# First adaptive norm of a 512-token network: modulation blocks summed along rows in PSUM, x/rms split off and computed ahead

## The chip, the cores and the metric

One core of one Trainium2 chip. The metric is the device time of one execution in microseconds (us); the kernel before has a median of 2411.16 us over three runs (2410.75 to 2412.59).

## What is computed

Two transformer-like networks one after the other on x (512 tokens, width 1024), four layers in all. The change touches only the beginning, the modulated norm of layer 0 and what the first projections need of it:

```python
def adaln(c, w_mod, b_mod):
    mod = jax.nn.silu(c) @ w_mod + b_mod
    return jnp.split(mod, 6, axis=-1)
...
def modulate(x, g, shift, scale):
    return rmsnorm(x, g) * (1.0 + scale[:, None, :]) + shift[:, None, :]
...
    sh_m, sc_m, g_m, sh_f, sc_f, g_f = adaln(c, mod_w, mod_b)
    h = modulate(x, norm_mix, sh_m, sc_m)
    (a_gate, a_x, q, kc, vc, ks, vs, kw, vw, gts) = _split(h @ w_in, IN0_SIZES)
```

c is one vector of 1024, so the modulation is a vector times a 1024 x 6144 matrix per layer. The first norm needs shift and scale, 16 blocks of 128 outputs (8 of each).

## The kernel before, in words

Activations lie transposed: partition = feature within a block of 128, eight blocks k, 512 tokens along the row. A product in fp32 quality is made of three products of rounded parts (`three`, L717: high x high, high x low, low x high), so every activation h is kept as h_hi and h_lo, and every weight panel (128 outputs x 1024 inputs) as w_hi and w_lo. SP loads raw panels into a ring of four; ScalarE copies the high part (L1233); GpSimd subtracts the low part (L640); TensorE multiplies (L718 to L720). The program is written out by hand for each of five engines, and semaphores order them.

The beginning: SP's queue issues the column constants, x, batch 0 of the modulation blocks (`first_mods`, 2 MB), raw panels 0 to 2, batches 1 to 3, raw panel 3. A batch n holds four blocks of 128 outputs: shift for k = 2n and 2n + 1, scale for the same two. ScalarE squares x (L1369), GpSimd adds the squares in pairs (L677), TensorE sums them over partitions (L952) and later spreads 1/rms over all partitions into bank 5 (`spread`, L820). ScalarE takes the root (L1374), VectorE its reciprocal (L1654).

In each batch TensorE multiplies block 0 with silu(c) as columns (L728, eight narrow products). VectorE sums blocks 1 to 3 over k in a chain of eight operations in PSUM (L1899, L1906), 384 elements each with a drain between, and TensorE sums the result over partitions (L732). `first_h(n)` (L1977) then adds the bias (L1980), makes the gain (L1984), scales x (tn, L1990), and after ScalarE's rounding (h_hi, L1259) subtracts the low part (L1995), for two k.

The order on VectorE is batch 0, reciprocal, batch 1, `first_h(0)`, `first_h(1)`, batches 2 and 3, `first_h(2)`, `first_h(3)`. On TensorE it is:

```python
            first_batch(0)
            spread(0, bank[5], QB)
            first_batch(1)
            by_k(0, h_hi, h_lo, 0, (0, 1, 2, 3))
            first_batch(2)
            first_batch(3)
            by_k(0, h_hi, h_lo, 0, (4, 5, 6, 7))
```

`by_k` (L735) multiplies panels 0, 1 and 2 side by side, nine products for each k as h_lo comes in. Behind it come panel 3, the products of `hidden(0)` (L978, from VectorE's blocks, L2052, and the weights w1), panel 4, the gates of the recurrence (L969, from VectorE's convolution, L2014 and L2017), and so on. ScalarE issues the loads of crow (a row of c on all partitions, for later blocks), peT, w2, w1, w_small and cmask after its last h_hi.

Of the kernel before, what the change touches and what calls it, by code (L numbers as in the profile page):

```python
# [13 lines left out]
F32 = mybir.dt.float32  # L14
# [105 lines left out]
def build(nc, A):  # L120
    with ExitStack() as ctx:
# [15 lines left out]
        FIRST_BANK = [bank[7], bank[4], bank[3], bank[7]]  # L137
        CHAIN = bank[6]
# [13 lines left out]
        modacc = sb("modacc", [P, 2])  # L152
        cols = sb("cols", [P, N_COLS])
# [34 lines left out]
        def s(name, shape, kib):  # L188
            return sb(name, shape, at=sx + int(kib * 1024))
# [5 lines left out]
        modsum = s("modsum", [P, 4, P], 16)  # L195
# [75 lines left out]
        crow_landed = sem("crow_landed")  # L271
        crow_ready = sem("crow_ready")
        first_landed = [sem(f"first_landed{n}") for n in range(BATCHES)]
        first_added = sem("first_added")
# [361 lines left out]
        def _(pool):  # L636
# [41 lines left out]
            split_from(0, P_OUT0 + 2)  # L678
# [37 lines left out]
        def _(pe):  # L716
# [17 lines left out]

# [212 lines left out]
            pe.wait_ge(csil_ready, 1)  # L947
            pe.wait_ge(filled, 1)
# [273 lines left out]
        def _(act):  # L1222
# [158 lines left out]
            act.wait_ge(mod_used, BATCHES)  # L1381
# [43 lines left out]
            for p in range(P_OUT0):  # L1425
# [188 lines left out]
        def _(dve):  # L1614
# [280 lines left out]
            def weighted(blocks_, n, to, used, between=None):  # L1895

                w = blocks_.rearrange("p n (k m) -> p n k m", m=P)
                part = CHAIN[:, 0:n * P].rearrange("p (n m) -> p n m", m=P)
                dve.tensor_scalar(part, w[:, :, 0, :], csil[:, 0:1], None, MUL)  # L1899
                for k in range(1, KB):  # L1900
                    if k == KB // 2 and between is not None:
                        between()
                    dve.drain()
                    if k == KB - 1 and used is not None:
                        dve.wait_ge(mod_used, used)
                    m = dve.scalar_tensor_tensor(out=part if k < KB - 1 else to, in0=w[:, :, k, :], scalar=csil[:, k:k + 1],  # L1906
                                                 in1=part, op0=MUL, op1=ADD)
                m.then_inc(mod_summed, 1)
                dve.drain()

            def sum_first(n, between=None):
                dve.wait_ge(first_landed[n], 16)
                weighted(first_mods[n][:, 1:4, :], 3, modsum[:, 1:4, :], n if n else None, between)
# [63 lines left out]
            def first_h(n):  # L1977

                dve.wait_ge(mod_used, n + 1)
                dve.tensor_tensor(by_part(modv[:, 0:2 * KB], n), FIRST_BANK[n][:, 0:4].rearrange("p (w k) -> p w k", w=2),  # L1980
                                  by_part(cols[:, COLS["modb"]:COLS["modb"] + 2 * KB], n), ADD).then_inc(first_added, 1)
# [3 lines left out]
                                         in1=cols[:, at:at + 2], op0=ADD, op1=MUL)  # L1985
                if n == 0:
                    dve.wait_ge(rstd_ready, 1)
                dve.drain()
                for k in (2 * n, 2 * n + 1):
                    dve.scalar_tensor_tensor(out=tn[:, k % 2, :], in0=x[:, k, :], scalar=gain(0, k), in1=bank[5][:, :],  # L1990
                                             op0=MUL, op1=MUL).then_inc(t_ready, 1)
                dve.drain()
# [569 lines left out]
```

## Time and profile before

| | us |
|---|---|
| median of three runs | 2411.16 |
| profiled execution | 2408.87 |
| its span | 2407.1 |
| TensorE busy | 2348.3 (98%) |
| VectorE busy | 1348.5 (56%) |
| ScalarE busy | 936.6 (39%) |
| GpSimd busy | 1123.0 (47%) |

The span is what the trace covers; the execution's own time is 1.8 us longer. Busy shares are averages over the whole program and say nothing of a single stage: for that one cuts the span into windows and reads the timelines. PE is TensorE's matmul, PEld its weight load, DVE VectorE, ACT ScalarE, POOL GpSimd, SP the engine that issues the panel loads; "ACTq" is an issue of a DMA by ScalarE's queue. Starts are counted from the start of the span. A row with x8 merges eight like instructions, its second number being the time from the first's start to the last's end, or nearly so.

### The profile page before, as it was taken

The page shows a single profiled execution, that of the slowest core. Times are in us where ns is not written, and L with a number is a line of the kernel's source. Part 1 is how long each engine was busy: PE and PEld are TensorE (multiplying, and loading weights), DVE is VectorE, ACT ScalarE, POOL GpSimd, SP SyncE. Part 2 cuts the span into 40 slices and gives each one's busy share as a digit, 9 for nine tenths or more (in the row PEclk, how much of TensorE's full clock was granted, in tenths as well). Part 3 has the DMA queues.
Part 4 walks back from the last instruction along what each step waited for, and adds up shares of the span by engine and source line. Part 5 has one row for each costly group of instructions (what it writes and reads, how often), then busy time and mean ns, then how long its engine had stood idle before and what let it go on. Part 6 is the DMA issues. An engine that isn't in the chain of part 4 may idle for free.

```text
span 2407.1 us, 33622 instructions
## 1 busy us (share of the span) xinstructions
PE 2348.3 (98%) x11781; PEld 1911.1 (79%) x11781; DVE 1348.5 (56%) x2132; ACT 936.6 (39%) x1495; POOL 1123.0 (47%) x529
## 2 busy tenths in 40 slices
PE   7999999999999999999999999999999999999998
PEld 6777788888776778888888678888888968888886
DVE  6786777772448651111158857263567474736455
ACT  3467332222336733222244544222256383322222
POOL 2346354554536535444446534444454473444443
PEclk9999999999999999999999999999999999999999
DMA  7530446653322023322332132323232202232322
GB/s 292 205 123 2 158 169 213 247 209 114 113 71 71 28 70 105 96 96 96 96 100 94 53 105 90 104 87 104 88 121 92 92 19 79 88 105 88 105 87 79
DMA packets 70095, 262.01 MB, mean 109 GB/s; under 512 B 7904, under 2 KB 8416, under 8 KB 68960
## 3 DMA queue, kind: packets, MB, share of 16 engines
q1 hardware_dynamic: 66816, 251.01, 30.8%
q10 hardware_dynamic: 3168, 9.50, 1.1%
q8 instruction: 72, 1.18, 0.2%
q14 instruction: 39, 0.32, 0.0%
HBM read 258.38 MB, written 2.10 MB: 108 GB/s over the span
## 4 chain that ended last, share of the span: by engine, by line
PE 88%; DVE 5%; issue 2%; POOL 1%; DMA 1%; ACT 1%; POOLq 1%; DVEq 0%; SPq 0%; ACTq 0%
PE bank L718 26%; PE bank L720 26%; PE bank L719 26%; PE bank L890 2%; PE bank L909 2%; PE bank L878 2%; POOL w_lo L640 1%; DMA first_mods<-in_first 1%; DVE acc L1646 1%; POOLq L706 1%; DVE bank L2254 1%; POOL prob L658 1%; PE bank L820 0%; DVE bank L1906 0%; DVE prob L1825 0%
## 5 line engine op out<-in xcount | busy, mean ns | idle before, releaser
L640 POOL TENSOR_TENSOR w_lo<-raw,w_hi 128x1024 fp32r<-128x1024 f32 x378 | 943.9, 2506 | 1178.9 <-ACT w_hi L1233 1176.9
L718 PE MATMUL bank<-h_hi,w_hi 128*128 128x512 f32 x1760 | 695.4, 395 | 12.3 <-DVE h_lo L1693 7.8
L719 PE MATMUL bank<-h_lo,w_hi 128*128 128x512 f32 x1760 | 688.9, 391 | 0.0
L720 PE MATMUL bank<-h_hi,w_lo 128*128 128x512 f32 x1760 | 688.9, 391 | 0.0
L1233 ACT ACTIVATE w_hi<-raw 128x1024 fp32r<-128x1024 f32 x378 | 392.6, 1051 | 426.8 <-PE bank L720 387.3
L718 PE MATMUL bank<-g_hi,w_hi 128*128 128x512 f32 x1072 | 421.1, 393 | 0.0
L720 PE MATMUL bank<-g_hi,w_lo 128*128 128x512 f32 x1072 | 420.9, 393 | 0.0
L719 PE MATMUL bank<-g_lo,w_hi 128*128 128x512 f32 x1072 | 417.3, 389 | 0.0
L718 PEld LDWEIGHTS bank<-h_hi,w_hi 128*128 128x128 f32 x1760 | 333.0, 189 | 93.4 <-DVE h_lo L1693 8.7
L720 PEld LDWEIGHTS bank<-h_hi,w_lo 128*128 128x128 f32 x1760 | 332.7, 189 | 70.4
L719 PEld LDWEIGHTS bank<-h_lo,w_hi 128*128 128x128 f32 x1760 | 333.2, 189 | 69.2 <-issue 0.8
L719 PEld LDWEIGHTS bank<-g_lo,w_hi 128*128 128x128 f32 x1072 | 201.3, 188 | 45.4
L720 PEld LDWEIGHTS bank<-g_hi,w_lo 128*128 128x128 f32 x1072 | 201.3, 188 | 45.2
L718 PEld LDWEIGHTS bank<-g_hi,w_hi 128*128 128x128 f32 x1072 | 201.5, 188 | 41.5 <-issue 0.2
L1785 DVE TENSOR_TENSOR prod<-silu,bank 128x512 f32<-128x512 f32 x44 | 30.2, 687 | 256.3 <-PE bank L720 253.8
L1919 DVE SCALAR_TENSOR_TENSOR modraw<-modraw,crow 128x1024 f32<-128x1024 f32 x80 | 160.4, 2034 | 22.1 <-DMA modraw<-in_blocks 21.3
L1298 ACT ACTIVATE g_hi<-prod 128x512 f32 x66 | 41.7, 632 | 303.9 <-DVE prod L1785 200.1
L658 POOL TENSOR_TENSOR prob<-prob,stat 128x256 f32<-128x256 f32 (+3 forms) x96 | 118.6, 1253 | 61.7 <-DVE stat L1834 42.7
L1709 DVE SCALAR_TENSOR_TENSOR x<-bank,plain,x 128x512 f32<-128x512 f32 x64 | 47.6, 749 | 155.7 <-PE bank L720 155.6
L1318 ACT ACTIVATE prob<-prob,stat 128x384 f32<-128x384 f32 (+2 forms) x192 | 105.9, 557 | 18.1 <-DVE stat L1825 17.5
L1709 DVE SCALAR_TENSOR_TENSOR x<-bank,modv,x 128x512 f32<-128x512 f32 x64 | 47.7, 749 | 112.9 <-PE bank L720 111.7
L1825 DVE CUSTOM_DVE_ANT_0 prob<-bank,mask 128x384 f32<-128x384 f32 (+2 forms) x192 | 86.0, 486 | 29.7 <-PE bank L878 28.5
(295 smaller groups left out, 2461.0 us busy)
## 6 DMA issues: line engine op xcount, KB each, us to landing
raw<-in_panels SPq DMA_DIRECT2D x378, 512.0 KB, 3.5
modraw<-in_blocks SPq DMA_DIRECT2D x80, 512.0 KB, 3.7
first_mods<-in_first SPq DMA_DIRECT2D x4, 2048.0 KB, 21.9
x<-in_x SPq DMA_DIRECT2D x1, 2048.0 KB, 8.3
w<-in_w ACTq DMA_DIRECT2D x1, 2048.0 KB, 8.7
out<-yout ACTq DMA_DIRECT2D x8, 256.0 KB, 2.2
mask<-in_causal ACTq DMA_DIRECT2D x1, 1024.0 KB, 5.0
mask<-in_dilated ACTq DMA_DIRECT2D x1, 1024.0 KB, 7.5
```

What stands on the lines that cost most here:

```text
L640: pool.tensor_tensor(w_lo[:, slot, :], raw[:, slot, :], w_hi[:, slot, :].bitcast(F32), ALU.subtract)\
L658: m = pool.tensor_tensor(both, both, stat[:, 2, u:u + 2].rearrange("p (b o) -> p b o", o=1) .broadcast_to((P, 2, w)), ALU.mult)
L718: pe.matmul(out, w_h, m_h, start=start, stop=False)
L719: pe.matmul(out, w_h, m_l, start=False, stop=False)
L720: return pe.matmul(out, w_l, m_h, start=False, stop=stop)
L878: m = pe.matmul(score_bank(run, n, b)[:, off:off + P * (i + 1)], q_of(run, i, c, b), k_of(run, i, c, br, b), start=True, stop=True)
L890: m = pe.transpose(bank[2 + b][:, P * j:P * j + P], prob[:, PROB_SLOT[n % PROB_STEPS], b, P * j:P * j + P], ident[:, :])
L1233: act.activation(w_hi[:, slot, :], raw[:, slot, :], ACT.Copy).then_inc(hi_ready, 1)
L1318: act.activation(row, row, ACT.Exp, bias=stat[:, 0, u:u + 1], scale=-1.0, accum_out=stat[:, 1, u:u + 1]).then_inc(exp_ready, 1)
L1709: dve.scalar_tensor_tensor(out=x[:, n, :], in0=bank[p % RING][:, :], scalar=scale_by, in1=x[:, n, :], op0=MUL, op1=ADD).then_inc(bank_free, 1)
L1825: dve.tensor_tensor_reduce(row_of(n, b, off, w), score_bank(run, n, b)[:, off:off + w], mask[:, i, 0:w], -SCALE, HIGHEST, ADD, ALU.min, st ...
L1919: dve.scalar_tensor_tensor(out=modraw[:, w, :], in0=modraw[:, w, :], scalar=1.0, in1=crow[:, :], op0=MUL, op1=MUL, accum_out=modacc[:, w:w ...
```

## The change

silu(c) is spread once over all partitions as a row in banks 6 and 7 (`spread_crow`, eight products with the identity). The modulation blocks are stored transposed (an output per partition), so VectorE gets a whole output with one multiplication along the row and an accumulator, in two halves of 512 since a bank holds 512 (`sum_rows`); of batches 1 to 3 block 0 stays with TensorE (`first_block`), of batch 0 all four are VectorE's. The sums over partitions (L732) are gone. x/rms is made once without the gain: k = 0, 1 by VectorE, k = 2 to 7 by GpSimd from a copy of 1/rms in SBUF. ScalarE applies gain and shift twice, to h_hi (rounded) and to the exact value in bank 3 or 5, and VectorE subtracts the two (`first_low`). ScalarE's table of roots is loaded ahead by a root of one. Its DMA issues come after the last exact value, lruw's among them, and crow is copied out of PSUM instead of loaded.

```diff
-        FIRST_BANK = [bank[7], bank[4], bank[3], bank[7]]
-        CHAIN = bank[6]
+        FIRST_COLUMN, FIRST_H = bank[4], (bank[3], bank[5])
+        CROW = (bank[6], bank[7])
...
-            split_from(0, P_OUT0 + 2)
+            split_from(0, 3)
+            pool.wait_ge(rb0_ready, 1)
+            for k in range(2, KB):
+                pool.tensor_tensor(sq0[:, k, :], x[:, k, :], rb0[:, :], ALU.mult).then_inc(xr_pool_ready, 1)
+            split_from(3, P_OUT0 - 1)
...
-            def first_batch(n):
+            def first_block(n):
 
                 pe.wait_ge(first_landed[n], 16)
-                if n == 3:
-                    pe.wait_ge(first_added, 1)
+                if n > 1:
+                    pe.wait_ge(mods_ready, n)
                 for k in range(KB):
-                    pe.matmul(FIRST_BANK[n][:, 0:1], first_mods[n][:, 0, P * k:P * k + P], csil[:, k:k + 1],
-                              start=(k == 0), stop=(k == KB - 1))
-                pe.wait_ge(mod_summed, n + 1)
-                for w in range(1, 4):
-                    m = pe.matmul(FIRST_BANK[n][:, w:w + 1], modsum[:, w, :], ones[:, 0:1], start=True, stop=True)
+                    m = pe.matmul(FIRST_COLUMN[:, n:n + 1], first_mods[n][:, 0, P * k:P * k + P], csil[:, k:k + 1],
+                                  start=(k == 0), stop=(k == KB - 1))
                 m.then_inc(mod_used, 1)
+
+            def spread_crow():
+
+                for k in range(KB):
+                    m = pe.matmul(CROW[k // 4][:, P * (k % 4):P * (k % 4) + P], csil[:, k:k + 1].broadcast_to((P, P)),
+                                  ident[:, :], start=True, stop=True)
+                m.then_inc(crow_spread, 1)
...
             pe.wait_ge(csil_ready, 1)
+            spread_crow()
...
-            first_batch(0)
             spread(0, bank[5], QB)
-            first_batch(1)
-            by_k(0, h_hi, h_lo, 0, (0, 1, 2, 3))
-            first_batch(2)
-            first_batch(3)
+            first_block(1)
+            by_k(0, h_hi, h_lo, 0, (0, 1))
+            first_block(2)
+            by_k(0, h_hi, h_lo, 0, (2, 3))
+            first_block(3)
             by_k(0, h_hi, h_lo, 0, (4, 5, 6, 7))
...
+            def first_high():
+
+                for k in range(KB):
+                    if k == 4:
+                        split_hi(3)
+                    act.wait_ge(mods_ready, k // 2 + 1)
+                    if k < 2:
+                        act.wait_ge(xr_ready, k + 1)
+                    else:
+                        act.wait_ge(xr_pool_ready, k - 1)
+                    act.activation(h_hi[:, k, :], sq0[:, k, :], ACT.Identity, bias=shift(0, k), scale=gain(0, k))\
+                        .then_inc(h_hi_ready, 1)
+                    if k == 1:
+                        act.wait_ge(rb0_ready, 1)
+                    elif k >= 2:
+                        act.wait_ge(h_lo_ready, k - 1)
+                    act.activation(FIRST_H[k % 2][:, :], sq0[:, k, :], ACT.Identity, bias=shift(0, k), scale=gain(0, k))\
+                        .then_inc(h32_ready, 1)
...
+            act.activation(root[:, 6 * QB - 1:6 * QB], one, ACT.Sqrt)
...
+            first_high()
+            act.wait_ge(h32_ready, KB)
             act.dma_start(lruw[:, :, :, :], A["lruw"]).then_inc(lru_landed, 16)
-            h_high(0)
-            act.dma_start(crow[:, :], A["crow"]).then_inc(crow_landed, 16)
...
-                    act.wait_ge(crow_landed, 16)
-                    act.activation(crow[:, :], crow[:, :], ACT.Silu).then_inc(crow_ready, 1)
+                    for half in range(2):
+                        m = act.activation(crow[:, T * half:T * half + T], CROW[half][:, :], ACT.Copy)
+                    m.then_inc(crow_ready, 1)
...
+            def sum_rows(n, ws):
+
                 dve.wait_ge(first_landed[n], 16)
-                weighted(first_mods[n][:, 1:4, :], 3, modsum[:, 1:4, :], n if n else None, between)
+                for w in ws:
+                    for half in range(2):
+                        row = first_mods[n][:, w, T * half:T * half + T]
+                        m = dve.scalar_tensor_tensor(out=row, in0=row, scalar=1.0, in1=CROW[half][:, :],
+                                                     op0=MUL, op1=MUL, accum_out=modhalf[:, half, w:w + 1])
+                if ws[-1] == 3:
+                    m.then_inc(mod_summed, 1)
...
+            def first_mod(n):
+
+                dve.drain()
+                if n:
+                    dve.wait_ge(mod_used, n)
+                    dve.tensor_copy(modhalf[:, 0, 0:1], FIRST_COLUMN[:, n:n + 1])
+                    dve.drain()
+                dve.tensor_tensor(modhalf[:, 0, :], modhalf[:, 0, :], modhalf[:, 1, :], ADD)
+                dve.drain()
...
+            def first_low(k):
+
+                dve.wait_ge(h_hi_ready, k + 1)
+                dve.wait_ge(h32_ready, k + 1)
+                dve.tensor_tensor(h_lo[:, k, :], FIRST_H[k % 2][:, :], h_hi[:, k, :].bitcast(F32), SUB).then_inc(h_lo_ready, 1)
+
+            dve.wait_ge(crow_spread, 1)
+            sum_rows(0, (0, 1, 2, 3))
             invert_root(0)
-            sum_first(1)
-            first_h(0)
-            first_h(1)
-            sum_first(2)
-            sum_first(3)
-            first_h(2)
-            first_h(3)
+            first_mod(0)
+            dve.wait_ge(rstd_ready, 1)
+            for k in range(2):
+                dve.tensor_tensor(sq0[:, k, :], x[:, k, :], bank[5][:, :], MUL).then_inc(xr_ready, 1)
+            dve.tensor_copy(rb0[:, :], bank[5][:, :]).then_inc(rb0_ready, 1)
+            for n in range(1, BATCHES):
+                ahead = (1,) if n == 1 else (1, 2)
+                sum_rows(n, ahead)
+                first_low(2 * n - 2)
+                first_low(2 * n - 1)
+                sum_rows(n, tuple(w for w in (1, 2, 3) if w not in ahead))
+                first_mod(n)
+            first_low(KB - 2)
+            first_low(KB - 1)
```

On VectorE, from the landing of batch 1 to the low parts of k = 0 and 1, before (modsum is the chain's result, tn the scaled x, bank7 batch 0's sums):

```order
L1899 TENSOR_SCALAR bank6<-first_mods1_80,csil_64 128x384 [waits first_landed1]
L1906 SCALAR_TENSOR_TENSOR bank6<-first_mods1_80,csil_64,bank6 128x384 x6
L1906 SCALAR_TENSOR_TENSOR modsum_84<-first_mods1_80,csil_64,bank6 128x384 [waits mod_used]
L1980 TENSOR_TENSOR modv_61<-bank7,cols_58 128x2x2 [waits mod_used]
L1984 SCALAR_TENSOR_TENSOR gains_62<-modv_61,cols_58 128x2
L1990 SCALAR_TENSOR_TENSOR tn_89<-x_49,gains_62,bank5 128x512 [waits rstd_ready]
L1990 SCALAR_TENSOR_TENSOR tn_89<-x_49,gains_62,bank5 128x512
L1995 SCALAR_TENSOR_TENSOR h_lo_51<-tn_89,modv_61,h_hi_50 128x512 [waits h_hi_ready] x2
```

and with the change (modhalf holds the half sums, sq0 x/rms, rb0 the copy of 1/rms, banks 3 and 5 the exact values):

```order
L2030 TENSOR_TENSOR sq0_84<-x_49,bank5 128x512 [waits rstd_ready]
L2030 TENSOR_TENSOR sq0_84<-x_49,bank5 128x512
L2031 COPY rb0_85<-bank5 128x512
L1933 SCALAR_TENSOR_TENSOR first_mods1_81,modhalf_58<-first_mods1_81,bank6 128x512 [waits first_landed1]
L1933 SCALAR_TENSOR_TENSOR first_mods1_81,modhalf_58<-first_mods1_81,bank7 128x512
L2022 TENSOR_TENSOR h_lo_51<-bank3,h_hi_50 128x512 [waits h32_ready,h_hi_ready]
L2022 TENSOR_TENSOR h_lo_51<-bank5,h_hi_50 128x512 [waits h32_ready,h_hi_ready]
L1933 SCALAR_TENSOR_TENSOR first_mods1_81,modhalf_58<-first_mods1_81,bank6 128x512 [waits first_landed1]
```

The low parts of k = 0 and 1 now stand behind two half rows of batch 1 instead of behind its whole chain, and the rest of batch 1 comes after them.

On ScalarE, between the squares and the first high part, before:

```order
L1233 ACTIVATE w_hi_53<-raw_52 128x1024 [waits raw_landed0]
L1233 ACTIVATE w_hi_53<-raw_52 128x1024 [waits raw_landed1]
L1233 ACTIVATE w_hi_53<-raw_52 128x1024 [waits raw_landed2]
L1374 ACT_TABLE_LOAD
L1374 ACTIVATE root_65<-bank0 128x1 [waits sums_ready]
```

and with the change:

```order
L1401 ACT_TABLE_LOAD
L1401 ACTIVATE root_66<-plain_64 128x1
L1247 ACTIVATE w_hi_53<-raw_52 128x1024 [waits raw_landed0]
L1247 ACTIVATE w_hi_53<-raw_52 128x1024 [waits raw_landed1]
L1247 ACTIVATE w_hi_53<-raw_52 128x1024 [waits raw_landed2]
L1406 ACTIVATE root_66<-bank0 128x1 [waits sums_ready]
```

The table load has moved from behind the three splits to ahead of them.

## Rows read from the trace of the kernel before

**Rows 1.** Windows: us, busy of each engine (instructions), granted clock, DMA.

```profile
0.00:70.00 70.00, 53.84 (x260) 48.27 (x261) 46.76 (x96) 26.70 (x38) 23.72 (x16) 0.95 0.74 290
...
1000.00:2407.00 1407.00, 1387.98 (x6751) 1140.03 (x6749) 732.01 (x1043) 523.25 (x762) 651.74 (x296) 0.99 0.27 90
```

**Rows 2.** Timeline of TensorE, first 75 us: start, us, line, operation.

```profile
12.20 6.96 PE L952 MATMUL bank<-ones,sq 128*128 128x1 f32 x32 [12.20 <-POOL sq L677]
...
23.71 2.05 PE L820 MATMUL bank<-ident,root 128*128 128x128 f32 x8
25.55 3.41 PE L728 MATMUL bank<-csil,first_mods 128*128 128x1 f32 x16
...
32.05 0.79 PE L718 MATMUL bank<-h_hi,w_hi 128*128 128x512 f32 x1 [1.45 <-DVE h_lo L1995]
...
36.06 0.42 PE L718 MATMUL bank<-h_hi,w_hi 128*128 128x512 f32 x1
...
42.23 1.84 PE L728 MATMUL bank<-csil,first_mods 128*128 128x1 f32 x16
...
50.33 0.79 PE L718 MATMUL bank<-h_hi,w_hi 128*128 128x512 f32 x1 [1.46 <-DVE h_lo L1995]
...
59.95 0.39 PE L718 MATMUL bank<-h_hi,w_hi 128*128 128x512 f32 x1
...
65.49 3.71 PE L978 MATMUL bank<-w,blocks 128*64 128x128 f32 x32
```

**Rows 3.** Timeline of VectorE, first 75 us.

```profile
14.55 0.62 DVE L1899 TENSOR_SCALAR bank<-first_mods,csil 128x384 f32<-128x384 f32 x1 [4.23 <-DMA first_mods<-in_first]
...
23.20 0.62 DVE L1899 TENSOR_SCALAR bank<-first_mods,csil 128x384 f32<-128x384 f32 x1 [1.95 <-DMA first_mods<-in_first]
...
29.46 0.16 DVE L1984 SCALAR_TENSOR_TENSOR gains<-modv,cols 128x2 f32<-128x2 f32 x1
29.71 1.41 DVE L1990 SCALAR_TENSOR_TENSOR tn<-x,gains,bank 128x512 f32<-128x512 f32 x2
...
58.87 5.60 DVE L2052 TENSOR_TENSOR blocks<-bank,peT 64x496 f32<-64x496 f32 x8 [4.04 <-PE bank L720]
...
71.83 0.68 DVE L1622 COPY axp<-bank 128x512 f32<-128x512 f32 x1
```

**Rows 4.** Timeline of ScalarE, first 75 us.

```profile
19.38 1.28 ACT L1374 ACT_TABLE_LOAD   x1
20.67 0.17 ACT L1374 ACTIVATE root<-bank 128x1 f32<-128x1 f32 x1
...
30.49 1.38 ACT L1259 ACTIVATE h_hi<-tn,modv 128x512 fp32r<-128x512 f32 x2 [9.46 <-DVE tn L1990]
...
52.99 0.33 ACTq L1378 DMA_DIRECT2D crow<-in_crow  x1
...
54.33 0.44 ACTq L1382 DMA_DIRECT2D w<-in_w  x1
```

**Rows 5.** Timeline of GpSimd, first 90 us.

```profile
10.78 4.94 POOL L677 TENSOR_TENSOR sq<-sq 128x512 f32<-128x512 f32 x4 [10.26 <-ACT sq L1369]
16.88 6.98 POOL L640 TENSOR_TENSOR w_lo<-raw,w_hi 128x1024 fp32r<-128x1024 f32 x3 [1.16 <-ACT w_hi L1233]
```

**Rows 6.** VectorE's groups, shapes apart (busy, mean ns); last row min/median/max ns.

```profile
L1919 DVE SCALAR_TENSOR_TENSOR modraw<-modraw,crow 128x1024 f32<-128x1024 f32 x80 | 160.4, 2034 | 22.1 <-DMA modraw<-in_blocks 21.3 <-issue 0.3
...
L1825 DVE CUSTOM_DVE_ANT_0 prob<-bank,mask 128x512 f32<-128x512 f32 x48 | 32.1, 686 | 10.9 <-PE bank L878 10.2 <-issue 0.4
...
L1785 DVE TENSOR_TENSOR prod<-silu,bank 128x512 f32<-128x512 f32 x44 | 30.2, 687 | 256.3 <-PE bank L720 253.8 <-issue 2.5
...
L1906 DVE SCALAR_TENSOR_TENSOR bank<-first_mods,csil,bank x24: 621/622/625, 15.3 to 46.1; 128x384 f32<-128x384 f32 x24
```

**Rows 7.** DMA issues, first 100 us: KB, us to landing.

```profile
w<-in_w ACTq DMA_DIRECT2D x1, 2048.0 KB, 8.7
```

**Rows 8.** Windows, as in the first group.

```profile
48.00:50.00 2.00, 0.88 (x5) 0.79 (x4) 1.87 (x3) 1.23 (x2) 0.00 (x0) 0.50 0.00 0
```

More of the change, by code:

```diff
@@ L152, in build @@
         modacc = sb("modacc", [P, 2])
+        modhalf = sb("modhalf", [P, 2, 4])
         cols = sb("cols", [P, N_COLS])
@@ L194, in build @@
         sq0 = s("sq0", [P, KB, T], 0)
-        modsum = s("modsum", [P, 4, P], 16)
+        rb0 = s("rb0", [P, T], 16)
         sq = s("sq", [P, 2, T], 0)
@@ L270, in build @@
         mod_landed = [sem(f"mod_landed{n}") for n in range(2)]
-        crow_landed = sem("crow_landed")
+        crow_spread = sem("crow_spread")
         crow_ready = sem("crow_ready")
         first_landed = [sem(f"first_landed{n}") for n in range(BATCHES)]
-        first_added = sem("first_added")
+        mods_ready = sem("mods_ready")
+        xr_ready = sem("xr_ready")
+        xr_pool_ready = sem("xr_pool_ready")
+        rb0_ready = sem("rb0_ready")
+        h32_ready = sem("h32_ready")
         consts_landed = sem("consts_landed")
@@ L1255, in h_high @@
                 for k in range(KB):
-                    if r == 0 and k == 4:
-                        split_hi(3)
-                    act.wait_ge(t_ready, KB * H_OF[r] + k + 1)
-                    act.activation(h_hi[:, k, :], tn[:, k % 2, :], ACT.Identity, bias=shift(r, k)).then_inc(h_hi_ready, 1)
+                    act.wait_ge(t_ready, KB * (H_OF[r] - 1) + k + 1)
+                    act.activation(h_hi[:, k, :], tn[:, k % 2, :], ACT.Identity, bias=shift(r, k)).then_inc(h_hi_ready, 1)
+            def first_high():
+                for k in range(KB):
+                    if k == 4:
+                        split_hi(3)
+                    act.wait_ge(mods_ready, k // 2 + 1)
[11 more added lines that the diff above has]
+                        .then_inc(h32_ready, 1)
             def project(p0, r):
@@ L1893, in set_gains @@
                 dve.drain()
[L1895 to L1911, printed above, removed]
-                dve.wait_ge(first_landed[n], 16)
-                weighted(first_mods[n][:, 1:4, :], 3, modsum[:, 1:4, :], n if n else None, between)
+            def sum_rows(n, ws):
+                dve.wait_ge(first_landed[n], 16)
+                for w in ws:
[5 more added lines that the diff above has]
+                    m.then_inc(mod_summed, 1)
             def sum_pair(m, landed):
@@ L1975, in by_part @@
                 return v_.rearrange("p (w k) -> p w k", w=2)[:, :, 2 * n:2 * n + 2]
[L1977 to L1981, printed above, removed]
+            def first_mod(n):
[6 more added lines that the diff above has]
+                dve.drain()
+                dve.tensor_tensor(by_part(modv[:, 0:2 * KB], n), modhalf[:, 0, :].rearrange("p (w k) -> p w k", w=2),
+                                  by_part(cols[:, COLS["modb"]:COLS["modb"] + 2 * KB], n), ADD)
+                if n == 0:
+                    dve.memset(modhalf[:, 1, 0:1], 0.0)
                 dve.drain()
@@ L1984, in first_h @@
                 dve.scalar_tensor_tensor(out=gains[:, 2 * n:2 * n + 2], in0=modv[:, KB + 2 * n:KB + 2 * n + 2], scalar=1.0,
[L1985 to L1991, printed above, removed]
@@ L1992, in first_h @@
-                dve.drain()
-                for k in (2 * n, 2 * n + 1):
-                    dve.wait_ge(h_hi_ready, k + 1)
-                    dve.scalar_tensor_tensor(out=h_lo[:, k, :], in0=tn[:, k % 2, :], scalar=shift(0, k),
-                                             in1=h_hi[:, k, :].bitcast(F32), op0=ADD, op1=SUB).then_inc(h_lo_ready, 1)
-                dve.drain()
-            dve.wait_ge(csil_ready, 1)
-            sum_first(0)
-            invert_root(0)
-            sum_first(1)
@@ L2003, in _ @@
[L2003 to L2008 removed]
+                                         in1=cols[:, at:at + 2], op0=ADD, op1=MUL).then_inc(mods_ready, 1)
+            def first_low(k):
+                dve.wait_ge(h_hi_ready, k + 1)
+                dve.wait_ge(h32_ready, k + 1)
+                dve.tensor_tensor(h_lo[:, k, :], FIRST_H[k % 2][:, :], h_hi[:, k, :].bitcast(F32), SUB).then_inc(h_lo_ready, 1)
@@ L2009, in _ @@
+            first_low(KB - 2)
+            first_low(KB - 1)
+            dve.drain()
             dve.memset(axp[:, :, 0:TAPS_LRU - 1], 0.0)
@@ L2479, in laid_out @@
     mods = np.concatenate([panel_arrays(f["l0_mod_w"]), panel_arrays(f["l1_mod_w"])])
-    out["first"] = np.stack([mods[[2 * n, 2 * n + 1, KB + 2 * n, KB + 2 * n + 1]] for n in range(BATCHES)]).transpose(0, 2, 1, 3)
     by_row = np.concatenate([f["l0_mod_w"].T, f["l1_mod_w"].T]).reshape(2 * MOD, P, D)
+    first_of = [[2 * n, 2 * n + 1, KB + 2 * n, KB + 2 * n + 1] for n in range(BATCHES)]
+    batches = [np.stack([by_row[b] if n == 0 or w else mods[b] for w, b in enumerate(of)]) for n, of in enumerate(first_of)]
+    out["first"] = np.stack(batches).transpose(0, 2, 1, 3)
     out["blocks"] = by_row[MOD_FIRST:]
-    out["crow"] = np.broadcast_to(f["c"], (P, D))
     def c(v_):
```

1 line of the change is left out of this document (removed).

## The prediction

> **What bounds the kernel now.** I read the windows first. After the first stage TensorE is the bound: from 1000 us on it is busy 1387.98 of 1407 us, but in the first 70 us only 53.84 [rows 1]. All that the change touches lies in those 70 us, and everything behind them hangs on TensorE's progress, so a microsecond by which the first real panel work ends earlier comes off the end.
>
> TensorE's timeline [rows 2] shows what it does there: column sums, narrow products of the modulation blocks, the spread of 1/rms, then panels 0 to 2 block by block in k. The first of these products starts at 32.05, a second pause lies between 42.23 and 50.33, and panel 3 starts at 59.95. That last moment is my mark. VectorE's timeline [rows 3] says who holds it up. Batch 0 begins when it lands (14.55), batch 1 when it lands (23.20), and only after all of batch 1 does it scale x (29.71), although the gains of k = 0, 1 hang on batch 0 alone. Later it sums batches 2 and 3 in one go before k = 4 is begun. The first stage is a chain of VectorE work with TensorE waiting.
>
> **The change, step by step.** The price of a half-row sum (128x512, one input in SBUF, one in PSUM, with an accumulator) is not in the trace. The nearest row is L1825, a custom operation with the same operands and an accumulator, 686 ns [rows 6]. The multiply that feeds prod from SBUF and PSUM takes 687 ns beside GpSimd's splits. Two operations one behind the other are some 0.05 to 0.09 us closer than their durations say (L1990: 1.41 us for two of 745 ns, [rows 3]). I take 0.66 us per half row. Upper bound: L1919, the same instruction over 1024 elements with both inputs in SBUF, means 2034 ns [rows 6], so 1.02 us per half; lower bound 0.61.
>
> Start of the norm. VectorE: 14.55 + 8 x 0.66 = 19.85. ScalarE's table load (1.28 us at 19.38, [rows 4]) goes ahead of the splits, into its wait for raw panel 0, so the roots start at 19.4, after the column sums (12.20 + 6.96 = 19.16, [rows 2]), and end at 19.75 instead of 21.03. Reciprocal by 20.1. The narrow products of batch 0 no longer stand ahead of the spread, so it runs from 20.15 and takes 2.05 [rows 2]: 22.2, against 25.76. The eight products of silu(c)'s row would cost about 4.1 (twice a spread), but stand where TensorE has nothing else to do until 12.20: nothing. The three small operations of batch 0's gains cost 0.26 each [rows 3], done before 22.2.
>
> k = 0. Multiply by 1/rms 22.3 to 23.0. ScalarE then writes high part and exact value: 0.73 + 0.65 (1.38 for two, [rows 4]) = 24.45. Writing to PSUM has no row; ScalarE's nearest are these. The Trainium skill (ScalarE: Activation LUTs, "Step-by-step: what each stage is for") calls PSUM the faster destination; by that the exact value would come a little sooner, no run here shows it. VectorE meanwhile: second product, copy of 1/rms (24.3), one row of batch 1 (25.6), low part 0.7: 26.3. TensorE has block 1's column in front: from 23.20 (landing) 3.5 us at the slow pace [rows 2], 26.7. So the products start at **26.8**, 5.25 earlier, bound by TensorE itself.
>
> The pace. In the trace the first nine products take 4.0 us (32.05 to 36.06), the rest 0.228 each [rows 2]. So k = 0, 1 (18 products) take 6.05: 32.85. Block 2's column at the fast pace 1.84: 34.7. VectorE: low(1) 26.95, four half rows 29.6, four small operations and a drain 1.15: 30.75; four half rows of batch 2 33.4; low(2) 34.1, ready before 34.7 (ScalarE's 1.4 us lie under the half rows). k = 2, 3: 18 x 0.228 = 4.1, 38.8. VectorE: low(3) 34.75, two half rows 36.1, small ones 37.2, so block 3's column runs 38.8 to 40.65. Four half rows 39.85, low(4) 40.5: k = 4, 5 from 40.65 to 44.75. VectorE: low(5) 41.2, two half rows 42.5, small ones 43.65; ScalarE two writes 45.05; low(6) 45.75. Here VectorE is late by 1.0. k = 6, 7: 45.8 + 4.1 = **49.9**. Mark: 59.95 - 49.9 = **10.05 us earlier**.
>
> GpSimd's six multiplies cost 1.24 each (4.94 for four additions, [rows 5]): from 24.3, k = 2 at 25.6, needed at 30.8; the last at 31.7. Behind them waits the split of panel 3 (2.3 us, a third of 6.98), whose low part is needed only at 49.9: hidden, with over 10 us to spare. The split's raw load and the later loads in SP's queue wait for the same low parts as before, at about the same time.
>
> What is late next. ScalarE's DMA issues follow its last write: 46.4 instead of 52.99 [rows 4], and lruw now goes ahead of the others instead of crow. w1 (2 MB) was issued at 54.33 and took 8.7 [rows 7], landing at 63.0, 10.0 after the first issue. Its first reader starts at 65.49, with 2.5 us to spare. That slack shrinks: the mark moves by 10.05, the issues by 6.6. The reader could start at 49.9 + 5.5 = 55.45; w1 lands at 46.4 + 10.0 = 56.4, or 55.7 with the 0.25 MB less ahead of it. A new wait of 0.25 to 0.95, I take **0.6**. The next one: VectorE's blocks take 5.6 [rows 3] and start at 49.7 when peT lands, the small weights come at about 56.3, the convolution ends near 64 against panel 4's end at 65.1, where before it had 3 us (71.83, [rows 3]). No wait, but thin.
>
> Sum: -10.05 + 0.6 = **-9.4 us**. Profiled execution 2408.87 to 2399.5; the median of the three runs stands 2.3 above it, so 2411.16 - 9.4 = **2401.8**.
>
> **Rivals.**
> (a) The clock drops in the gaps. Between 48 and 50 us the granted clock is 0.50, the lower of the two levels, after some 4.5 us of nothing but narrow products [rows 8], and 50.33 starts slowly. The gaps now are 1.85, 1.85 and 1.0 us, all shorter. If the clock fell nevertheless at both columns, k = 2, 3 would end at 40.65, the slow column takes it to 42.5 or 44.2, and 36 products with a slow start need 10.0: mark at 52.5 to 54.2, gain 5.7 to 7.4, time near 2404.5. The Trainium skill (TensorE: Matmul & The Clock Gate, "What's actually happening") lets the clock fall after an idle window that runs freely; the trace agrees that a long narrow stretch does it. By it a gap this short should be safe, unless narrow products and pauses together count as idle.
> (b) VectorE is the bound throughout, since half rows cost more. Adding up its chain gives the mark as 32.8 + 26 p (26 half rows of p us; 49.95 at 0.66). At p = 0.85 the gain is 5.05 less the 0.6: within the 0.2% (4.8 us), which is what a measurement of this kernel can tell from no change. At the upper bound 1.02 the mark is 59.3, nothing gained: 2411. Against: every operation with a PSUM input in rows 6 is near 0.69.
> (c) Slower. GpSimd holds VectorE up at the SBUF port, PSUM input or not. L1919's mean of 2034 shows such holds where both inputs are in SBUF. GpSimd works from 16.88 to 23.86 (6.98, [rows 5]) and then its 7.4 us of multiplies, which stand beside half rows now and beside nothing before. If every operation of VectorE waited for one of GpSimd, it would lose up to 7.0 + 7.4 = 14.4: mark at 64.3, and the end at 2415 to 2416. It decides from 10 us of loss on. Against it: L1906 reads SBUF and PSUM and is 621 to 625 ns over all 24, those beside the splits of 16.88 among them [rows 6]. The Trainium skill (SBUF — State Buffer, "Who interferes with whom") says a VectorE instruction with at most one SBUF input doesn't contend; the trace agrees, with these 621 to 625 ns. By it this rival would be out.
> (d) The gain is given back behind the mark: w1, w_small or the convolution 3 to 5 us late, or VectorE and GpSimd falling into worse step in the attention. Then 2405 to 2407. For it: three slacks shrink at once.
>
> **Chances.** Forecast 0.70, (a) 0.14, (b) 0.06 with half of it inside 0.2%, (c) 0.03, (d) 0.07 with half inside. Faster by over 0.2%: 0.90; within: 0.07; slower: 0.03. Range: below, no VectorE delay at k = 6 and no wait for w1 give a mark of 48.9, -11.05 us, 2400.1, and 1 us for the spread of the runs: 2399.0. Above, (a) and half of (d): 2406.4.
>
> **What would show it.** The first h_hi,w_hi product at 26.8; L1933 near 0.69 us; pauses of TensorE before k = 2 and 4 under 0.3 us and before k = 6 about 1; panel 3 at 49.9; hidden(0) waiting for w1 by 0.6; the granted clock at 1.00 from 31 us on. Half rows of over 0.8 us would mean (b) or (c), products of 0.43 us after 34 us (a), an unchanged distance from mark to end is what I count on, and any growth of it over 1.5 us is (d).

## The result: 10.5 us slower, though the first stage ends 6.9 us earlier

| | before | after |
|---|---|---|
| median of five runs, us | 2411.62 | 2422.10 |
| lowest to highest | 2410.75 to 2413.54 | 2420.76 to 2427.55 |
| span of the profiled execution | 2407.1 | 2419.0 |

The ratio is 1.0042 (95% interval 1.0031 to 1.0054). The forecast was 2401.8.

The windows of the changed kernel's trace answer to [rows 1]; two stretches are added, in which TensorE has nothing but products of g_hi and g_lo (columns: from and to, length, busy us and instructions of PE, PEld, DVE, ACT, POOL, granted clock, DMA share, GB/s).

```profile
0.00:70.00 70.00, 55.61 (x264) 47.25 (x264) 50.42 (x123) 32.71 (x49) 31.76 (x23) 0.85 0.75 292
400.00:420.00 20.00, 20.00 (x87) 16.09 (x86) 15.33 (x19) 3.19 (x3) 9.06 (x4) 1.00 0.78 270
1890.00:1900.00 10.00, 10.00 (x85) 10.00 (x85) 5.02 (x5) 2.00 (x2) 3.46 (x2) 1.00 0.18 55
1000.00:2407.00 1407.00, 1394.06 (x6733) 1137.91 (x6731) 723.65 (x1032) 521.56 (x759) 652.13 (x296) 1.00 0.27 89
```

The same two stretches of the kernel before:

```profile
400.00:420.00 20.00, 20.00 (x89) 16.43 (x88) 15.03 (x20) 3.18 (x3) 8.10 (x4) 1.00 0.76 259
1890.00:1900.00 10.00, 10.00 (x91) 10.00 (x90) 6.76 (x4) 2.01 (x2) 5.20 (x2) 1.00 0.34 107
```

TensorE is busy without a gap and its clock is granted in full in both, yet 87 of its instructions fall into 20 us where 89 did, and 85 into 10 us where 91 did. Over the last 1407 us it is busy 6.08 us more for 18 instructions fewer. So the loss is not waiting: the products themselves follow each other more slowly. The durations of single products don't show it well (0.39 to 0.40 us each, since they overlap); the distance from start to start does. Rows of TensorE's timeline, first of the kernel before, then of the changed one:

```profile
399.91 0.39 PE L718 MATMUL bank<-g_hi,w_hi 128*128 128x512 f32 x1
...
419.82 0.39 PE L718 MATMUL bank<-g_hi,w_hi 128*128 128x512 f32 x1
```

```profile
399.95 0.39 PE L727 MATMUL bank<-g_hi,w_hi 128*128 128x512 f32 x1
...
420.25 0.40 PE L727 MATMUL bank<-g_hi,w_hi 128*128 128x512 f32 x1
```

Between the two rows lie 87 products each time: 19.91 / 87 = 228.9 ns before, 20.30 / 87 = 233.3 ns after. I call this distance the pace. Taken so over the whole trace (9264 products of panels), the pace is 226.7 ns in both kernels where h_hi and h_lo are the moving operand and nothing interrupts. Where g_hi and g_lo move it is 228.9 and 233.3. And where g_hi is held still and 256 columns of w_hi move (near 1900 us) it is 113.3 and 120.0. Added up from 300 us on, the slower pace is 15.4 us (over the whole trace the mean with g_hi and g_lo moving is a little lower than in these rows, 229.0 and 233.0).

**The first stage** did about what was forecast. TensorE's timeline after, answering to [rows 2]:

```profile
4.56 3.78 PE L744 MATMUL bank<-ident,csil 128*128 128x128 f32 x16 [4.56 <-ACT csil L1395]
12.16 6.96 PE L966 MATMUL bank<-ones,sq 128*128 128x1 f32 x32 [3.82 <-POOL sq L682]
...
27.73 0.80 PE L727 MATMUL bank<-h_hi,w_hi 128*128 128x512 f32 x1 [1.05 <-DVE h_lo L2022]
...
36.77 0.50 PE L727 MATMUL bank<-h_hi,w_hi 128*128 128x512 f32 x1 [0.77 <-DVE h_lo L2022]
...
43.66 0.50 PE L727 MATMUL bank<-h_hi,w_hi 128*128 128x512 f32 x1 [0.83 <-DVE h_lo L2022]
...
48.84 0.50 PE L727 MATMUL bank<-h_hi,w_hi 128*128 128x512 f32 x1 [0.82 <-DVE h_lo L2022]
...
53.07 0.39 PE L727 MATMUL bank<-h_hi,w_hi 128*128 128x512 f32 x1
...
59.30 3.71 PE L992 MATMUL bank<-w,blocks 128*64 128x128 f32 x32 [0.64 <-DMA w<-in_w]
```

The granted clock's mean is 0.85 over these 70 us, and 0.95 in [rows 1]. A window of the kernel before, then of the changed one:

```profile
20.00:28.00 8.00, 8.00 (x40) 8.00 (x39) 4.18 (x9) 1.02 (x5) 3.86 (x2) 1.00 1.01 423
```

```profile
20.00:28.00 8.00, 5.74 (x25) 5.36 (x26) 7.77 (x13) 2.90 (x4) 5.87 (x4) 0.50 1.00 427
```

The record stays at 0.50 until 32 us and is 1.00 from 34 us on, where I forecast 1.00 from 31. Yet the column sums take 6.96 us in both kernels, and the first products begin 0.43 us apart in both (27.73 to 32.16 here, 32.05 to 36.06 before), nearly twice the later 0.23. So the two records differ where the work does not, and no time of this stage hangs on that. The mark (panel 3) is at 53.07 instead of 59.95: 6.9 us earlier, where 10.05 were forecast. hidden(0) starts at 59.30 instead of 65.49 and waits 0.64 us for w1, as forecast (0.6). TensorE pauses before each of the four groups of k, and the row says for whom: VectorE. Only the last of these pauses, before k = 6, was forecast, at about 1. Its timeline after, without the half rows (L1933), answers to [rows 3]; GpSimd's, beneath it, to [rows 5]:

```profile
19.85 1.67 DVE L2007 TENSOR_TENSOR modhalf<-modhalf 128x4 f32<-128x4 f32 x1
21.60 2.22 DVE L2009 TENSOR_TENSOR modv<-modhalf,cols 128x4 f32<-128x4 f32 x1
...
31.20 1.00 DVE L2007 TENSOR_TENSOR modhalf<-modhalf 128x4 f32<-128x4 f32 x1
32.27 1.17 DVE L2009 TENSOR_TENSOR modv<-modhalf,cols 128x4 f32<-128x4 f32 x1
...
38.94 1.15 DVE L2007 TENSOR_TENSOR modhalf<-modhalf 128x4 f32<-128x4 f32 x1
40.17 0.17 DVE L2009 TENSOR_TENSOR modv<-modhalf,cols 128x4 f32<-128x4 f32 x1
...
45.83 0.16 DVE L2007 TENSOR_TENSOR modhalf<-modhalf 128x4 f32<-128x4 f32 x1
```

```profile
16.83 6.97 POOL L645 TENSOR_TENSOR w_lo<-raw,w_hi 128x1024 fp32r<-128x1024 f32 x3 [1.12 <-ACT w_hi L1247]
25.94 7.49 POOL L686 TENSOR_TENSOR sq<-x,rb 128x512 f32<-128x512 f32 x6 [2.13 <-DVE rb L2031]
37.67 2.40 POOL L645 TENSOR_TENSOR w_lo<-raw,w_hi 128x1024 fp32r<-128x1024 f32 x1 [4.25 <-ACT w_hi L1247]
```

Additions of four numbers per partition take 1.0 to 2.2 us while GpSimd works, and each of the five ends where an operation of GpSimd ends: 23.82 beside 23.80, 33.44 beside 33.43, 40.09 beside 40.07, and the other two, taken apart from the merged rows, 21.52 beside 21.50 and 32.20 beside 32.18. At 40.17 and 45.83 GpSimd is idle, and such an addition takes 0.16 to 0.17. They read two tensors in SBUF. The half rows, with one input in SBUF and one in PSUM, are not touched:

```profile
L1933 DVE SCALAR_TENSOR_TENSOR first_mods<-first_mods,bank 128x512 f32<-128x512 f32 x26 | 16.3, 682 | 4.3 <-DMA first_mods<-in_first 4.3
```

So there are two things to settle: why products that the change doesn't touch go slower, and whether the small additions are what the first stage lacks.

### The profile page after: what moved, and what is told of

Its sections match the earlier page's. It is cut to its first block, busy times and chain, and to the rows that moved or that the text cites. A ratio compares the mean times of both kernels' runs of the same rounds, so it can differ in the third digit from the quotient of the medians.

```text
span 2419.0 us, 33590 instructions
## 1 busy us (share of the span) xinstructions
PE 2358.0 (97%) x11757; PEld 1906.9 (79%) x11757; DVE 1340.6 (55%) x2155; ACT 942.2 (39%) x1504; POOL 1130.2 (47%) x535
## 4 chain that ended last, share of the span: by engine, by line
PE 85%; DVE 6%; issue 3%; DMA 2%; POOL 1%; ACT 1%; POOLq 1%; DVEq 1%; SPq 0%; ACTq 0%
PE bank L727 26%; PE bank L728 26%; PE bank L729 26%; PE bank L903 2%; PE bank L922 2%; PE bank L891 2%; DMA modraw<-in_blocks 1%; POOL w_lo L645 1%; DVE acc L1678 1%; POOLq L715 1%; DVE bank L2287 1%; DMA raw<-in_panels 1%; DVE modraw L1942 1%; POOL prob L663 1%; DVE xc L2050 1%
## 5 line engine op out<-in xcount | busy, mean ns | idle before, releaser
L728 PE MATMUL bank<-g_lo,w_hi 128*128 128x512 f32 x1072 | 423.2, 395 | 0.0
```

Of the source, the lines that this page charges most:

```text
L728: pe.matmul(out, w_h, m_l, start=False, stop=False)
```

## The experiments

**First four: is it the place in TensorE's instruction stream?** My first theory for the pace. The changed kernel issues fewer instructions on TensorE, so all code behind stands elsewhere in the stream, and the pace differed in stretches that are not loops. Each kernel gets extra narrow products where TensorE is idle, 12 of them making up for the difference:

```diff
+            pe.wait_ge(filled, 1)
+            for _ in range(12):          # or 1, or 4
+                pe.matmul(bank[4][:, 8:9], ones[:, :], ones[:, 0:1], start=True, stop=True)
             pe.wait_ge(csil_ready, 1)
```

> Twelve narrow products more on TensorE in the changed kernel, before csil is ready, where TensorE has nothing to do; their results are read by nobody. They bring the number of TensorE's instructions ahead of everything behind the first stage back to about that of the kernel before. Theory L (the place of the straight-line code in TensorE's instruction stream sets its pace): first stage as in the changed kernel, panel 3 at 53.1 +- 0.3 us; the 192 products from about 377 us on go at 228.9 ns each, no longer 233.2, the narrower ones of attention(2) at 113.3 instead of 120.0; time 2404 to 2409. Rival W (the changed work itself, or where tiles and loads now stand in time, slows the later products): pace stays 233.2 and 120.0, time 2420 to 2424.

> The same with one narrow product more instead of twelve. Theory L: the first stage is unchanged, and the pace of the straight-line stretches may differ from 233.2 ns in some or all of them; time anywhere from 2404 to 2424, by how many of them change. Rival W: 2420 to 2424 and 233.2 ns.

> Four narrow products more in the kernel before, in the same idle time of TensorE. Theory L: panel 3 at 59.95 as before, the pace of the straight-line stretches may leave 228.9 ns; time 2408 to 2426. Rival W: 228.9 ns, 2410.7 to 2413.5 as before.

> Twelve narrow products more in the kernel before. Theory L: panel 3 at 59.95, the pace of the straight-line stretches may leave 228.9 ns; time 2408 to 2426. Rival W: 228.9 ns, 2410.7 to 2413.5.

| kernel | median, us | ratio to before (95%) | pace with g_hi moving / held |
|---|---|---|---|
| after, 12 more | 2423.78 | 1.0047 (1.0030 to 1.0064) | 233.3 / 120.0 |
| after, 1 more | 2423.18 | 1.0040 (1.0026 to 1.0054) | 233.3 / 120.0 |
| before, 4 more | 2413.47 | 1.0002 (0.9993 to 1.0012) | 228.9 / 113.3 |
| before, 12 more | 2414.59 | 1.0004 (0.9994 to 1.0014) | 228.9 / 113.3 |

Theory L falls: no padding moves the pace in any of these stretches. The rival W, that the changed work or its moment slows the products, is not yet shown either.

**Second four: the SBUF address.** What the slow stretches have in common is the tile: they read g_hi and g_lo. These are allocated behind modacc, and the change puts a new tile, modhalf, between. It is 32 bytes per partition, rounded up to 64, so that g_hi and all behind it stand 64 B higher, while h_hi and the weights' ring stand as before. This one line of the diff moved the tiles, and the prediction never looked at it. Four kernels move g_hi in steps of 64 B, in either version, and with it all tiles allocated behind the moved one; no instruction differs otherwise:

```diff
-        modhalf = sb("modhalf", [P, 2, 4])        # e2_after_same_place
 ...
         sp = sb("sp", [P, 6, LC])
+        modhalf = sb("modhalf", [P, 2, 4])        # and modacc too: e2_after_m64
```
```diff
         modacc = sb("modacc", [P, 2])
+        hole = sb("hole", [P, 16])                # e2_before_p64; behind modhalf: e2_after_p64
```

> The new small tile modhalf (64 B per partition) stands behind all others instead of ahead of cols, so that every tile behind it, g_hi and g_lo (the moving operands of the down and out panels) and attention's tiles among them, has the SBUF address that it has in the kernel before; nothing else differs from the changed kernel. Theory A (the SBUF address of the moving tiles sets the pace): the 192 products from about 377 us on at 228.9 ns, no longer 233.2; attention(2)'s at 113.3 instead of 120.0; panel 3 at 53.1; time 2405 to 2410, below the kernel before. Rival W (the changed work itself slows the later products): 233.2 and 120.0, 2420 to 2424.

> The kernel before with 64 B per partition left empty behind modacc, so that the tiles behind it have the addresses of the changed kernel; no instruction differs otherwise. Theory A: 233.2 ns and 120.0 from 380 us on, panel 3 at 59.95, time 2424 to 2429 (15 us of pace more). Rival W: 228.9 and 113.3, 2410.7 to 2413.5.

> As e2_after_same_place, and modacc (64 B) behind all others too: the tiles behind stand 64 B lower than in the kernel before. Theory A says that the pace depends on the address, not by how much: between 226.7 ns (that of the products whose moving tile is h_hi, 128 B past a multiple of 16 KB, as g_hi now is past a multiple of 1 KB) and 233.2; if 226.7, the time is 2398 to 2405. Rival W: 233.2, 2420 to 2424.

> The changed kernel with a further 64 B left empty behind modhalf: g_hi 64 B higher than there. Theory A: the pace is another than 233.2 ns or the same, by the period in the address; if it only matters whether the address is a multiple of 128 B (as in the changed kernel) or not (as before), 228.9 and 2405 to 2410. Rival W: 233.2, 2420 to 2424.

| kernel | g_hi against before | median, us | ratio to before (95%) | pace moving / held |
|---|---|---|---|---|
| after, same place | 0 | 2408.84 | 0.9982 (0.9972 to 0.9992) | 228.9 / 113.3 |
| before, +64 B | +64 | 2427.16 | 1.0051 (1.0034 to 1.0068) | 233.3 / 120.0 |
| after, -64 B | -64 | 2404.40 | 0.9957 (0.9941 to 0.9974) | 226.7 / 120.0 |
| after, +64 B | +128 | 2422.43 | 1.0033 (1.0020 to 1.0046) | 233.3 / 117.8 |

W, which forecast unchanged paces in all four, falls by the first three. Theory A holds in the first two, whose paces and times it named. For the last two it left the pace open: 226.7 was its lower bound for the third, and the guess that all depends on whether g_hi stands at a multiple of 128 B (228.9 for the fourth) missed. A hole of 64 B in the kernel before, without an instruction changed, costs 13.9 us (2427.16 against 2413.25) and brings the changed kernel's paces. With its tiles back in place the changed kernel is faster than before. The window of 400 to 420 us, of the kernel before with its hole, then of the changed one with g_hi 64 B lower:

```profile
400.00:420.00 20.00, 20.00 (x87) 16.12 (x86) 15.00 (x19) 3.18 (x3) 8.22 (x4) 1.00 0.71 236
```

```profile
400.00:420.00 20.00, 20.00 (x90) 16.57 (x89) 14.63 (x19) 3.19 (x3) 8.17 (x4) 1.00 0.78 265
```

87 instructions in the first, as in the changed kernel; 90 in the second. Such a count is coarse, since products overlap and those cut by an edge are counted too. By the starts the second kernel has 226.7 ns here, the pace that its h_hi panels have.

**Last four: one address or a distance, and the small additions.** Two are the kernel before, one with modacc behind all other tiles, so that g_hi stands 64 B lower, one with all tiles 64 B higher; the third rewrites the small additions in the changed kernel with g_hi 64 B lower; the fourth is its base.

```diff
-        base = (nc.sbuf_base + 63) // 64 * 64
+        base = (nc.sbuf_base + 63) // 64 * 64 + 64        # e3_before_all64
```
```diff
-                dve.tensor_tensor(modhalf[:, 0, :], modhalf[:, 0, :], modhalf[:, 1, :], ADD)        # e3_m64_cols
-                dve.drain()
-                dve.tensor_tensor(by_part(modv[:, 0:2 * KB], n), ..., by_part(cols[...], n), ADD)
+                for w in range(4):
+                    dve.tensor_scalar(to, modhalf[:, 0, w:w + 1], modhalf[:, 1, w:w + 1], cols[:, own:own + 1], ADD, ADD)
                 dve.drain()
-                dve.scalar_tensor_tensor(out=gains[:, 2 * n:2 * n + 2], ...)
+                for k in (2 * n, 2 * n + 1):
+                    dve.tensor_scalar(gains[:, k:k + 1], modv[:, KB + k:KB + k + 1], 1.0, cols[:, at:at + 1], ADD, MUL)
```

> The kernel before with modacc behind all other tiles, so that g_hi and all tiles behind it stand 64 B lower, as in e2_after_m64; nothing of the change. Theory A (address of the tiles that TensorE reads sets its pace): down panels at 226.7 ns for 228.9, the 384 narrower products of the last stretch at 120.0 for 113.3; 2880 products or so gain 2.2 ns (6.3 us), 384 lose 6.7 (2.6 us): 2407 to 2410 where the kernel before gives 2411 to 2413. Rival (address and change act only together): as the kernel before.

> The kernel before with every tile 64 B higher, x, h_hi and the weights' ring too: distances between tiles as before, every address another. Theory A1 (what counts is how the moving and the stationary tile stand to each other): 226.7 ns where h_hi is read, 228.9 for g_hi, 113.3 at 1900 us, and the time of before, 2410 to 2415. Theory A2 (what counts is each tile's own address): paces of 228.9 to 233 where h_hi is read, too, over some 5000 products: 2420 to 2450.

> e2_after_m64 with the small operations of the gains written without a second tensor in SBUF: each column is one tensor_scalar (half sum, plus the other half as its scalar, plus the modulation's constant as the other), two more for the gains, and one drain fewer. Theory P (the pauses before k = 0, 2, 4, 6 come from small operations with two SBUF tensors that wait for GpSimd's): each of these takes under 0.3 us, first product at 26.5 to 27.0, pauses before k = 2 and 4 under 0.3 us, panel 3 at 50.5 to 51.5 for 53.1; hidden(0) then waits 1 to 2 us for w1, and the end comes 0.5 to 2 us earlier than that of e2_after_m64. Rival Q (any VectorE operation waits there, whatever it reads): the columns take 0.5 to 2 us as a group beside GpSimd's work as the old ones did, panel 3 at 53 or later.

> e2_after_m64 once more, for the comparison on one chip with the kernels of this job: 2402.5 to 2405.5; 0.9957 of the kernel before, within 0.0015; 5 +- 2 us below e3_before_m64, by the mark's 6.9 less what is given back.

| kernel | median, us | ratio to before (95%) | pace h_hi / g_hi moving / g_hi held |
|---|---|---|---|
| before, g_hi -64 B | 2408.48 | 0.9981 (0.9972 to 0.9990) | 226.7 / 226.7 / 120.0 |
| before, all +64 B | 2412.78 | 0.9998 (0.9989 to 1.0007) | 226.7 / 228.9 / 113.3 |
| after, g_hi -64 B, small columns | 2400.16 | 0.9947 (0.9933 to 0.9960) | 226.7 / 226.7 / 120.0 |
| after, g_hi -64 B | 2403.34 | 0.9960 (0.9947 to 0.9974) | 226.7 / 226.7 / 120.0 |

*Address.* With everything 64 B higher all paces stay, though every tile has another address: A2 falls at this step, and what counts is a distance between tiles, A1. That the distance is the one to the weights, the other tile that TensorE reads, is argued and not shown, since the other tiles ahead of g_hi stay in place as well; h_hi speaks for it (below the table). The kernel with g_hi 64 B lower came out as expected, in paces and time. By the allocations, g_hi stands past w_hi by a number of kilobytes and these bytes over:

| bytes over a multiple of 1 KB | 0 | 64 | 128 | 192 |
|---|---|---|---|---|
| which | g_hi -64; also h_hi in all | before | after | after, +64 |
| g moves, w held (512 columns), ns | 226.7 | 228.9 | 233.3 | 233.3 |
| w moves, g held (256 columns), ns | 120.0 | 113.3 | 120.0 | 117.8 |

h_hi, 0 bytes over in every kernel, has 226.7 when it moves and 120.0 when it is held, as g_hi has at 0. What inside the chip makes it so, and what the period is, these runs don't say: only four steps of 64 B were tried, and each figure is a mean over products whose own starts are 0 or 512 B further apart (the block of k starts 512 k bytes into its weight panel and 2048 k bytes into g_hi). Single distances of the changed kernel alternate between about 230 and 236 ns.

*Small additions.* VectorE's timeline of e3_m64_cols, the place that answers to 19.85 above, and the group of all of them:

```profile
19.93 0.27 DVE L2012 TENSOR_SCALAR modv<-modhalf,cols 128x1 f32<-128x1 f32 x1
20.39 0.64 DVE L2016 TENSOR_SCALAR modv<-modhalf,cols 128x1 f32<-128x1 f32 x3 [0.19 <-issue]
21.11 0.33 DVE L2020 TENSOR_SCALAR gains<-modv,cols 128x1 f32<-128x1 f32 x2
```

```profile
L2016 DVE TENSOR_SCALAR modv<-modhalf,cols x12: 263/265/273, 20.4 to 42.6; 128x1 f32<-128x1 f32 x12
```

Twelve operations of 263 to 273 ns: nine fall beside GpSimd's splits and multiplies (16.90 to 23.88, 23.96 to 31.41 and 35.81 to 38.21 here), three beside an idle GpSimd (264 to 267 ns). Nothing is held up. TensorE's timeline of the same kernel:

```profile
45.65 0.50 PE L727 MATMUL bank<-h_hi,w_hi 128*128 128x512 f32 x1 [0.29 <-DVE h_lo L2027]
...
49.87 0.39 PE L727 MATMUL bank<-h_hi,w_hi 128*128 128x512 f32 x1
...
56.33 3.71 PE L992 MATMUL bank<-w,blocks 128*64 128x128 f32 x32 [0.86 <-DMA w<-in_w]
```

One pause is left of the four, 0.29 us, and panel 3 starts at 49.87, where the forecast had 49.9. Theory P holds in its mechanism and Q falls. Its numbers behind the first product were missed, all to the better: the mark moves by 3.3 us (53.20 in e3_after_m64) to below the expected 50.5 to 51.5, the wait for w1 grows from 0.5 to 0.86 where 1 to 2 were expected, and the end comes 3.2 us earlier (2400.16 against 2403.34), where I expected 0.5 to 2. I had taken too long a wait for w1, whose issue moves along with the mark. Against the kernel before at the same addresses, on the same chip, it is 8.3 us (2400.16 against 2408.48). It is the fastest of all that ran: 2400.16, 0.9947 of before.

**What the change alone is worth**, read at equal addresses: 4.4 us faster at 64 bytes over (2408.84 against 2413.25), 5.1 at 0 (2403.34 against 2408.48), less surely at 128, 5.1 by the medians (2422.10 against 2427.16) but 2.2 by the ratios (1.0042 against 1.0051), as the two were measured on different occasions. The address costs it 13 to 15: 13.3 by the medians (2422.10 against 2408.84), 14.5 by the ratios (1.0042 less 0.9982), 15.4 by the starts.

## Why the prediction was wrong, step by step

- **Bound and path.** "Everything behind them hangs on TensorE's progress, so a microsecond by which the first real panel work ends earlier comes off the end." This is the step that failed. It holds while the pace behind is unchanged. The change moved g_hi by 64 B, which some 3200 wide products read (1072 of each of the three kinds in the profile's groups, 4.4 ns each: 14.2 us) and 384 narrow ones (6.7 ns each: 2.6 us); the starts show 15.4 of these 16.8. Against that stands the gain of some 4 to 5 us that the change brings at equal addresses, where 9.4 were forecast. None of the rivals had the pace. (c) forecast a loss, 2415 to 2416, by another mechanism, and the measured 2422 lies outside it too.
- **Half rows, 0.66 us each.** The group's durations are 682 ns and starts 0.61 apart: 0.05 better than taken, so (b) is out.
- **Start of the norm.** Products forecast from 26.8, measured 27.73; 26.7 once the additions were rewritten. ScalarE's first pair took 1.48 us (24.76 to 26.24) for the 1.38 priced, its writes to PSUM 0.76 each beside 0.80 to 0.82 for those to SBUF; the spread took 2.08 for 2.05.
- **Small operations, "0.26 each".** The term that was mis-sized: 3.9 us for the first two, then 2.2 and 1.3. It makes up the miss of 3.2 us at the mark (53.07 against 49.9): with the additions rewritten the mark is 49.87. That this meets 49.9 so closely is partly luck. In that kernel twelve products go at the slow pace where nine were priced so (26.67 to 31.93), 0.4 late at k = 2, and the cheaper half rows left a pause of 0.3 before k = 6 where 1 was forecast. The price came from [rows 3], where the operation ran while GpSimd was idle. The trace of before did hold a warning, in a group that I hadn't read:

```profile
L1925 DVE TENSOR_TENSOR modv<-modacc,cols x40: 160/164/2384, 83.6 to 555.7; 128x2 f32<-128x2 f32 x24, 128x2 f32 x16
```

  Two elements per partition, median 164 ns, at most 2384. Nineteen of the 40 take 1.95 to 2.38 us, and each of these ends within 0.03 us of a split of GpSimd.
- **Rival (c), half right.** I asked whether GpSimd holds up operations that read PSUM. It doesn't: 682 ns for 26 half rows. I weighed one SBUF input for these, and never asked the same of the operations with two, which stood in the sum at 0.26. The Trainium skill (SBUF — State Buffer, "Who interferes with whom") says that a VectorE instruction with at most one SBUF input, outside its modes that use both ports, does not contend with GpSimd, and that one with two SBUF inputs contends with a GpSimd instruction that reads SBUF. Both sets of rows agree. That section doesn't say how scalars from SBUF count; the columns of e3_m64_cols, with one SBUF tensor and up to two such scalars, were not held up.
- **w1.** Forecast wait 0.6, measured 0.64; issues at 46.4 forecast, 49.43 measured, late by the same 3 us as the mark.
- **Rival (a).** In the changed kernel's profile no product behind 33 us is slow: out. In the profile of e2_after_m64 the granted clock was 0.94 from 40 to 44 us and 0.64 from 44 to 48, and some products began 0.43 us apart; its panel 3 still started at 53.6, so the price there was about 0.4 us (53.2 in e3_after_m64, the same kernel).
- **Rival (d), given back behind the mark.** The lead is 6.2 us at hidden(0) and 3.9 at 240 us. With equal addresses some 6.7 at the mark became 4.4 at the end (1.9 to 6.8 by the interval). Part of it is seen as a lower granted clock where before has none. Windows of before, then of after:

```profile
174.00:182.00 8.00, 5.62 (x38) 3.43 (x40) 7.36 (x33) 8.00 (x29) 7.66 (x6) 1.00 0.01 2
768.00:776.00 8.00, 5.36 (x34) 2.73 (x30) 7.08 (x28) 6.74 (x19) 5.56 (x3) 1.00 0.22 66
```

```profile
174.00:182.00 8.00, 6.92 (x46) 4.27 (x48) 4.16 (x18) 5.03 (x16) 5.10 (x6) 0.79 0.01 3
768.00:776.00 8.00, 5.36 (x29) 3.25 (x28) 7.43 (x35) 6.76 (x21) 5.13 (x3) 0.82 0.22 66
```

  0.21 and 0.18 of 8 us, up to 1.7 and 1.4 us. Both stand behind pauses that both kernels have. But the first is not the change's doing. Three kernels without the change, e2_before_p64, e3_before_m64 and e3_before_all64, show the same fall in their profiles, and lose the same 1.6 us against before between 172 and 240 us. The window of e3_before_all64, the stage being a little later there:

```profile
182.00:190.00 8.00, 8.00 (x60) 5.04 (x61) 4.16 (x15) 4.66 (x14) 4.00 (x4) 0.79 0.01 2
```

  Their marks stand at 61.2 to 61.4, too, against 59.95 in the profile of before, which is of one of its faster executions (2408.87; the medians run from 2411.62 to 2413.27). So a difference of up to 1.6 us between one profile and one other says nothing of the change. e1_after_pad12's profile had a full clock at 174 us and a lead of 5.3 at 240, but it had 3.6 left at 311 us, and its median is no lower. How much is really given back, and whether such falls are all of it, stays open; no run took them away.

## What to carry to other kernels

A new tile is a change to everything allocated behind it. Before a change is judged, put new tiles behind all others, or compare the starts of untouched matmuls in both traces; and if a kernel is bound by TensorE, shift its moving tiles against its stationary ones in steps of 64 B, which was worth 4.8 us here without any other edit and could cost 14. A small operation on VectorE that reads two SBUF tensors beside GpSimd's work is priced by what GpSimd is doing (1.0 to 2.4 us here), not by its own length (0.16).

## What the runs showed that I had not expected

- The pace of back-to-back products at the full clock depends on how far apart tiles stand in SBUF, by all that fits the two tiles that the product reads: 226.7 to 233.3 ns for 512 columns, 113.3 to 120.0 for 256, and the best distance is not the same for both (0 bytes over for the one, 64 for the other).
- The tensor_scalar form with both scalars taken from SBUF, so three SBUF operands in all, was not held up in any of the nine cases beside GpSimd's work (263 to 273 ns), while the tensor_tensor of 4 elements was in all five beside it (the other three of its eight fell beside an idle GpSimd).
